# Dilated-attention keys and values to token rows: another queue for the value stores, four staging slots for keys, bias tables flipped in mid-stage

## The reference, cut to what matters

```python
logits = jnp.einsum('bqhd,bqkhd->bqhk', q, kk).astype(jnp.float32) * HEAD_DIM ** -0.5
logits = jnp.where(valid[None, :, None, :], logits + bias[None, None], -jnp.inf)
...
bufs = tuple(jnp.stack([k_a[:, -min(w, S):, g], v_a[:, -min(w, S):, g]], axis=2)
             for g, (w, _) in enumerate(DSA_GROUPS))
```

## Time and profile before

| | |
|---|---|
| runs (us) | 2523.01, 2510.16, 2494.77; median 2510.16 |
| profiled execution | 2512.98 us; span of its instructions 2511.2 us |
| busy share of the span | PE 89%, DVE 42%, ACT 21%, POOL 3% |
| mean granted TensorE clock | 0.913 |
| changed stage in the span | 377.6 to 402.1 us, some 24.5 us of 2511.2 |
| prompt attention behind it | 402.1 to about 530 us |

### The profile page before, as it was taken

The page is one execution under the profiler, slowest core; times in us unless marked ns, Lnnn a source line. Parts: engine busy times, 40 slices in busy tenths (PEclk is TensorE's granted clock), DMA queues, the critical chain, the costliest instruction groups (busy, mean ns, idle before and its releaser), DMA issues. The chain is left out here.

```text
span 2511.2 us, 40144 instructions
## 1 busy us (share of the span) xinstructions
PE 2228.1 (89%) x17448; PEld 1962.4 (78%) x17448; DVE 1061.6 (42%) x1398; ACT 523.0 (21%) x954; POOL 71.5 (3%) x129
## 2 busy tenths in 40 slices
PE   6999978957899788885899989777999999999997
PEld 6999966835577555554788888657999999999996
DVE  4212134565466577771222232566432432422433
ACT  3101004421333233230111121224111110111110
POOL 0000000000400011100000000000000000000000
PEclk8999957658899899996899999987999999999998
DMA  5113132031695378864211111301111111111111
GB/s 185 42 50 119 25 102 86 26 91 31 200 331 192 139 274 300 305 252 117 106 46 46 52 34 31 127 19 32 45 51 43 51 44 47 45 51 43 50 43 76
DMA packets 179012, 247.98 MB, mean 99 GB/s; under 512 B 23219, under 2 KB 164507, under 8 KB 173516
## 3 DMA queue, kind: packets, MB, share of 16 engines
q1 hardware_dynamic: 166992, 162.04, 20.8%
q0 software_dynamic: 5904, 83.95, 8.8%
q10 hardware_dynamic: 5996, 0.25, 0.2%
HBM read 220.35 MB, written 69.87 MB: 116 GB/s over the span
## 5 line engine op out<-in xcount | busy, mean ns | idle before, releaser
L1158 PE MATMUL ps<-mla_rt,q_now 32*32 32x256 f32 x4608 | 148.9, 396 | 48.5 <-DVE mla_rt L1252 44.3
L1252 DVE STREAM_TRANSPOSE mla_rt<-mla_rows 128x1536 f32<-128x1536 f32 x96 | 164.7, 1752 | 43.5 <-DMA mla_rows<-in_cache_mla,page_rows 43.0
L2306 PE MATMUL ps<-xn_hi,mlp_w_hi 128*128 128x344 f32 x768 | 164.1, 322 | 7.2 <-DVE mlp_w_lo L2120 5.3
L2306 PE MATMUL ps<-mlp_xn_lo,mlp_w_hi 128*128 128x344 f32 x768 | 163.7, 321 | 0.0
L1158 PEld LDWEIGHTS ps<-mla_rt,q_now 32*32 32x32 f32 x4608 | 97.1, 108 | 84.4 <-issue 63.1
L2306 PE MATMUL ps<-u_lo,mlp_w_hi 128*128 128x344 f32 x768 | 163.0, 320 | 0.0
L2306 PE MATMUL ps<-xn_hi,mlp_w_lo 128*128 128x344 f32 x768 | 162.9, 320 | 0.0
L2306 PE MATMUL ps<-u_hi,mlp_w_hi 128*128 128x344 f32 x768 | 162.9, 320 | 0.0
L2306 PE MATMUL ps<-u_hi,mlp_w_lo 128*128 128x344 f32 x768 | 162.1, 319 | 0.0
L2306 PEld LDWEIGHTS ps<-xn_hi,mlp_w_hi 128*128 128x128 f32 x768 | 129.7, 190 | 8.7 <-DVE mlp_w_lo L2120 6.4
L2306 PE MATMUL ps<-xn_hi,win_hi 128*128 128x344 f32 x576 | 123.3, 323 | 7.9 <-DVE win_lo L2571 7.9
(11 more groups left out here) (368 smaller groups left out, 3756.8 us busy)
## 6 DMA issues: line engine op xcount, KB each, us to landing
out_s_dsa_w<-in_cache_dsa_w SPq DMA_DIRECT2D x8, 4094.0 KB, 80.2
oaT<-in_w_up SPq DMA_DIRECT2D x32, 512.0 KB, 4.1
oaT<-in_w_down SPq DMA_DIRECT2D x32, 512.0 KB, 4.2
obT<-in_w_in SPq DMA_DIRECT2D x23, 512.0 KB, 3.7
gate_w<-in_w_in SPq DMA_DIRECT2D x16, 512.0 KB, 4.1
out_s_dsa_w<-in_cache_dsa_w SPq DMA_DIRECT2D x8, 1022.0 KB, 17.6
s_kv_tile<-in_cache_dsa_w SPq DMA_DIRECT2D x12, 512.0 KB, 5.5
x_scr<-qkvT SPq DMA_DIRECT2D x1, 4128.0 KB, 15.9
```

The source lines that it names most:

```text
L1158: last = nc.tensor.matmul(ps[32 * (JG * s + g):32 * (JG * s + g) + 32, i, 0:JN * SQ], q_now[SQ * i:SQ * i + SQ, s, c, :], rt[SQ * i:SQ * i ...
L1252: nc.vector.transpose(rt[:, k * n:(k + 1) * n], rows[:, v, :, k * n * SQ:(k + 1) * n * SQ].rearrange("p n (c f) -> p c n f", c=n)).then_in ...
L2306: last = nc.tensor.matmul(out[:, t, 0:TC], w, x[:, k, t * TC:(t + 1) * TC], start=first, stop=stop)
```

## The change

The value stores leave SyncE's queue for GpSimd's, with a semaphore of their own (`v_stored`), on which GpSimd waits in the merge at the end of the attention. The keys have four staging slots instead of two. The first four flips stand before unit 4's transposes and the fifth before unit 8's; the copies of the tables stand before ScalarE's copy of unit 5 (table 0), behind VectorE's second key copy (table 1), and before ScalarE's copy of unit 12 (tab2). The fifth flip uses the bank that the first table's copy has left.

```diff
+    v_stored = sem("v_stored")
...
-        kst = sb(st, "kst", [P, 2, GW])
+        kst = sb(st, "kst", [P, 4, GW])
...
-        k_stored = [sem("k_stored0"), sem("k_stored1")]
+        k_stored = [sem(f"k_stored{s}") for s in range(4)]
+        tab_moved = sem("tab_moved")
...
             @block.tensor
             def _(pe):
+                flip = mats[:, C_FLIP:C_FLIP + P]
                 for u, (g, i, q, _prev, _d) in enumerate(units):
                     if u >= 2:
                         pe.wait_ge(copied, u - 1)
+                    if u == 4:
+                        pe.wait_ge(tab_in, 16 * 3)
+                        for n in range(4):
+                            last = nc.tensor.matmul(ps[:, 2 + n, :], flip,
+                                                    sc[:, n // 2, 2 * (n % 2):2 * (n % 2) + 2, :].rearrange("p h n -> p (h n)"),
+                                                    start=True, stop=True)
+                        last.then_inc(flipped, 1)
+                    if u == 8:
+                        pe.wait_ge(tab_moved, 1)
+                        nc.tensor.matmul(ps[:, 2, :], flip, pt[:, 0, :, 0, :], start=True, stop=True).then_inc(flipped, 1)
...
-                flip = mats[:, C_FLIP:C_FLIP + P]
-                pe.wait_ge(tab_in, 16 * 3)
-                for n in range(4):
-                    nc.tensor.matmul(ps[:, 2 + n, :], flip, sc[:, n // 2, 2 * (n % 2):2 * (n % 2) + 2, :].rearrange("p h n -> p (h n)"),
-                                     start=True, stop=True).then_inc(flipped, 1)
-                pe.wait_ge(k_copied, len(kunits))
-                nc.tensor.matmul(ps[:, 6, :], flip, pt[:, 0, :, 0, :], start=True, stop=True).then_inc(flipped, 1)
             @block.scalar
             def _(act):
                 for u in range(NUN):
+                    if u == 5:
+                        act.wait_ge(flipped, 1)
+                        nc.scalar.activation(tab01[:, 0].rearrange("p h n -> p (h n)"),
+                                             ps[:, 2:4, :].rearrange("p a n -> p (a n)"), ACT.Copy).then_inc(tab_moved, 1)
+                    if u == 12:
+                        act.wait_ge(flipped, 2)
+                        nc.scalar.activation(tab2[:].rearrange("p h n -> p (h n)"), ps[:, 2, :], ACT.Copy)
                     act.wait_ge(turned, u + 1)
                     nc.scalar.activation(vtok[:, u, :], ps[:, u % 2, 256:512], ACT.Copy).then_inc(copied, 1)
-                for g in range(2):
...
-                act.wait_ge(flipped, 5)
-                nc.scalar.activation(tab2[:].rearrange("p h n -> p (h n)"), ps[:, 6, :], ACT.Copy)
             @block.vector
             def _(dve):
                 for n, u in enumerate(kunits):
                     dve.wait_ge(turned, u + 1)
-                    if n >= 2:
-                        dve.wait_ge(k_stored[n % 2], n // 2 * 16)
-                    nc.vector.tensor_copy(kst[:, n % 2, :], ps[:, 6 + n % 2, 0:GW]).then_inc(k_copied, 1)
+                    if n >= 4:
+                        dve.wait_ge(k_stored[n % 4], n // 4 * 16)
+                    nc.vector.tensor_copy(kst[:, n % 4, :], ps[:, 6 + n % 2, 0:GW]).then_inc(k_copied, 1)
+                    if n == 1:
+                        dve.wait_ge(flipped, 1)
+                        nc.vector.tensor_copy(tab01[:, 1].rearrange("p h n -> p (h n)"),
+                                              ps[:, 4:6, :].rearrange("p a n -> p (a n)"))
+            @block.gpsimd
+            def _(pool):
+                for u in kunits:
+                    g, i = units[u][:2]
+                    pool.wait_ge(copied, u + 1)
+                    pool.dma_start(rows_of(g, i, 1), vtok[:, u, :]).then_inc(v_stored, 16)
             @block.sync
             def _(sp):
...
                 for n, u in enumerate(kunits):
                     g, i = units[u][:2]
-                    sp.wait_ge(copied, u + 1)
-                    sp.dma_start(rows_of(g, i, 1), vtok[:, u, :]).then_inc(s_out, 16)
-                    n_out[0] += 1
                     sp.wait_ge(k_copied, n + 1)
-                    sp.dma_start(rows_of(g, i, 0), kst[:, n % 2, :]).then_inc(k_stored[n % 2], 16)
-                for s in range(2):
-                    sp.wait_ge(k_stored[s], 16 * ((len(kunits) + 1 - s) // 2))
+                    sp.dma_start(rows_of(g, i, 0), kst[:, n % 4, :]).then_inc(k_stored[n % 4], 16)
+                for s in range(4):
+                    sp.wait_ge(k_stored[s], 16 * ((len(kunits) + 3 - s) // 4))
...
+            @block.gpsimd
+            def _(pool):
+                pool.wait_ge(v_stored, 16 * len(kunits))
```

More of the change, by code:

```diff
@@ L392, in _ @@
                 for u in range(NUN):
+                    if u == 5:
[5 more added lines that the diff above has]
+                        nc.scalar.activation(tab2[:].rearrange("p h n -> p (h n)"), ps[:, 2, :], ACT.Copy)
                     act.wait_ge(turned, u + 1)
                     nc.scalar.activation(vtok[:, u, :], ps[:, u % 2, 256:512], ACT.Copy).then_inc(copied, 1)
-                for g in range(2):
-                    act.wait_ge(flipped, 2 * g + 2)
-                    nc.scalar.activation(tab01[:, g].rearrange("p h n -> p (h n)"),
-                                         ps[:, 2 + 2 * g:4 + 2 * g, :].rearrange("p a n -> p (a n)"), ACT.Copy)
-                act.wait_ge(flipped, 5)
-                nc.scalar.activation(tab2[:].rearrange("p h n -> p (h n)"), ps[:, 6, :], ACT.Copy)
             @block.vector
```

## The result

The change made the kernel slower by a little: 2513.82 us against 2503.32 us (medians of 20 runs each), 10.5 us apart. The ratio worked out from all these runs is 1.0036 with a 95% interval of 1.0023 to 1.0050, which is 9 us, between 6 and 12.5. The profiled execution spans 2519.1 us against 2511.2.

A forecast was written before the change was run, and what follows sets the result against it. Key slots and the flips at the end were taken to cost time in a stage of 24.6 of 2511.2 us. Wait 3.95, flips 5.15, units 4 to 16 +1.3, last leg -6.0 gave +4.4: 2514.5 us, range 2500 to 2528.

The forecast's parts named there:

- The wait at unit 4: TensorE stands at unit 4 until the third table load lands, wholly on the path: 3.95 us, bounds 3.6 and 4.45.
- Four flips: Eight flip instructions at unit 4, partly at half clock: 5.15 us, bounds 3.4 and 6.9.
- the rival: Half clock stays: four flips take 6.9 us, plus fifth flip and units 9 to 15; +7.8 in all, 2518; chance 0.10.
- Unit 4 to unit 16: Fifth flip and table copies lengthen this leg from 7.46 us to 8.8: +1.3, bounds +0.5 and +2.5.
- The last leg: Unit 16 to the next stage shrinks from 14.73 us to 8.7 with four slots: -6.0, bounds -7.6 and -4.8.
- eight units take 6.0 us: From unit 16 on, stores at 352 GB/s set the pace: 0.75 us a unit, so 6.0 us for eight.
- The sum: The four terms of the stage together: 3.95 + 5.15 + 1.3 - 6.0 = +4.4 us, bounds -0.1 and +9.05.
- The price of an issue: GpSimd gets thirteen value stores at 0.58 us a plain issue, keeping up with 0.75 us a unit.
- GpSimd ends the stage: Rival: issues of 1.24 us hold GpSimd at the barrier, +2.5 us more, +6.9 in all, 2517; chance 0.13.
- the bound at which bandwidth doesn't count: Unit 16 to the next stage if bandwidth didn't bind: 7.1 us, which gives -7.6.
- the attention would gain from a shifted clock: Rival: the attention behind the stage gains clock; with 20 us to full clock the sum is -5.6, 2504.6; chance 0.17.
- the change does less than it says: Rival: the keys' pace stays at 1.14 us, last leg only -2.5, sum +7.9, 2518; chance 0.05.

The follow-up runs named there:

- e3: The change with the value stores back on SyncE's queue: stage 30.7 us against the change's 31.3.
- e6: The change with the wait at unit 4 kept and the four flips there left out but for one narrow product: stage 26.9 us against the change's 31.3.
- e7: The change with five more flips of other data behind TensorE's last transposes, keeping it busy until the stage ends: stage 30.7 us against the change's 31.3.
- e5: The change with the four flips reading other data, so nothing is waited for at unit 4 (tables waited for at unit 8): stage 25.8 us against 31.3.
- e9: The change with flips before units 17, 19, 21, table copies on ScalarE, the last key stores waited for in the attention: stage 23.2 us, ratio to before 0.9987.
- e11: As e9, without the drain that GpSimd runs before the barrier at the stage's end: stage 20.6 us against e9's 23.2.
- e4: The change with the flips moved from units 4 and 8 to units 10 and 14, table copies moved along: stage 24.9 us against the change's 31.3.
- e10: As e9, with the value stores put back on SyncE's queue: stage 21.9 us against e9's 23.2.
- e2: The kernel before with four key slots alone, value stores on SyncE's queue and flips at the end: stage 21.2 us against 24.5, ratio 1.0004.
- e12: Thirteen key slots, no store waits in the stage, value stores at the attention's start, four value banks, flips at units 12, 16, 20: stage 18.5 us, ratio 0.9986.

## Why the prediction was right, and where its terms were off

**The hit on the total is in part luck.** 2514.5 us was forecast and 2513.8 measured, but the forecast started from 2510.2, the median of three runs, and the median of twenty is 2503.3. Added to that, +4.4 gives 2507.7. A base 6.8 us too high made up for an effect that was put too small. What was right by its mechanism is the sign (the flips' move costs more than the slots give back), the wait, and that it all stays within 1%.

**The wait at unit 4** was the term that decides, and it was there: 4.36 us instead of 3.95. The third load took 5.2 us to land, not 4.9; e3, e6 and e7 waited 4.1. TensorE ran nothing past it: no instruction in the 4.36 us, and unit 4's transposes only behind the flips. e5 shows that it is a cost by itself.

**Four flips** were put at 5.15 us, and the stretch took 5.96. The course was right (clock 0.50 from 382.92 to 388.70, then 1.00). The size of 3.35 us at half clock came from one row; here the clock came up 5.8 us into the flips, so nearly all of them ran at half clock, as the rival had it. The rival's price for them, 6.9 us, counted eight spacings of 0.86; counted between loads the first spacing is about 0.2. Its further terms did not come: from 388.88 on the clock was 1.00. But the same flips took 4.9 us in e3 and 5.7 in e7, both behind a stand-still, and 4.9 in e5 without one. So 5.15 lies within what the runs show, and what makes the clock rise sooner or later here stays open. The stand-still isn't needed for a slow start either: in the kernel before the clock was at 0.50 too from 377.50 to 383.00, past unit 4.

**Unit 4 to unit 16** took 8.15 us, +0.7 and not +1.3. Units 4 to 9 took 4.7 us (4.6 worked out) and units 10 to 15 3.5 (4.2): it is the copy to tab2 that hid better than worked out.

**The last leg** is the term that was sized worst: 10.5 us (397.03 to 407.50) and not 8.7, so it gave back 4.3 us and not 6.0. The step was "eight units take 6.0 us" at 352 GB/s, a rate read from a quarter of a microsecond. Over 397.03 to 401.00 it was 257 GB/s and then, to 404.30, 314. And the stretch moved 2.67 MB, where eight units are 2.10: stores of the units before unit 16 were still under way or not yet begun. Stores then landed in 2.9 to 3.1 us, so four slots filled up again (VectorE's last copy waited 1.48 us). That bandwidth would take over from the slots was right from 401.00 on (DMA share 0.97; before that 0.78). Behind the last landing the step had 0.3 us; 407.50 is 0.65 us behind the last key (404.75 and 2.1 us), because GpSimd was not at the barrier yet (below).

**The sum** of the four is 4.36 + 5.96 + 0.69 - 4.26 = +6.75 us for the stage (the wait is new, so it counts whole) where +4.4 was forecast. It lies inside the measured 6 to 12.5. Two more profiles of the same front, e3 and e7, have 6.2. The other 2 us are not settled: the attention was 2.6 us longer in this profile, but by e7 and the table that is within its own scatter.

**GpSimd's stores.** The price of an issue was near: 0.54 us for 0.58, thirteen times, with VectorE's key copies beside them, and the last of seven in a row (397.98 to 402.09) started 0.3 us behind its copy, so no backlog. The later wait costs nothing: GpSimd's last store landed at 406.68, and the merge starts at 537.5. What the prediction didn't have is the barrier's wait for GpSimd's landings (e9, e11). It costs little in the change, but it does set the end there. The last value store, issued at 403.58, landed after 3.1 us at 406.68, and the next stage started 0.8 us behind it, as in e4 to e9. The last key landed at 406.85, and in e3, where GpSimd has no stores, the next stage starts 0.4 us behind the last key (406.49 and 406.89). That would be 407.25, so the wait is worth some 0.25 us, an estimate from these rows. The rival named the right place (GpSimd ends the stage) with the wrong cause, issue time, and at ten times the price. With both queues at work, 401.00 to 404.30, GpSimd's took 52.8% of the 16 DMA engines and SyncE's 44.4%, together 0.97 at 314 GB/s; SyncE's alone had reached 1.03 and 352 GB/s before. So no road of its own shows for GpSimd: the last leg gave back 4.3 us, not the 7.6 of the bound at which bandwidth doesn't count. What its queue saves is issue time: that sets e3's last leg, 11.2 us against 10.5. In e10 and e11 the saving is seen again: 21.9 us against 20.6.

**The other rivals.** That the attention would gain from a shifted clock was given 0.17; with a scatter of 12 us between profiles it can be neither claimed nor excluded from one. That the change does less than it says is refuted: VectorE's waits for slots halved, and e2 shows 3.4 us for the slots.

## What to carry to other kernels

Before a wait is moved forward in an engine's list, read when its event lands, not when it was last needed: here a load that had been 12 us early became 4.4 us late, in which TensorE ran nothing at all, and the work moved so far forward ran at a lower clock as well (3.2 us for the same flips at unit 10 at 0.96, 6.0 at unit 4 in the change at 0.52). A bundle of three edits hid a good one (slots, -3.4 us of stage) under a bad one (flips, +10.4), which running each alone shows at once. Two runs that differ in one edit are best compared leg by leg: e3's stage was 0.6 us shorter than the change's while the leg that the edit touches was 0.8 us longer. And where stores go to GpSimd's queue, read its drain at the stage's end: here it waited for them, 3.2 to 3.7 us against 34 ns without stores, though the kernel asks for them only in the merge.

## What the runs showed of the hardware that was not expected

- With its drain, GpSimd joined the barrier only after its own stores had landed: the next stage started 0.8 us behind the last landing in e9 (395.5 + 2.6 = 398.1, end of the 3.18 us drain 398.7, start 398.91); without the drain it started 0.4 us behind ScalarE's last copy (395.65 and 396.06) and 0.07 us behind the end of GpSimd's last issue (395.99), which may be what held it. SyncE's outstanding stores didn't hold the barrier in e10: the stage ended 0.42 us after its last issue, which took 1.9 us to land, and SyncE's drain took 0.12 us.
- After 4.1 to 4.4 us without work TensorE's clock stayed at 0.50 until 3.7 (e3), 5.2 (e7) or 5.8 us (the change) into the same continuous flips; with work ahead of them it rose 3.7 us into the flips (e5).
- The same attention stage took between 118.0 and 130.0 us in fourteen profiles, its mean granted clock between 0.60 and 0.76. The code of its engines is the same but for waits and stores put into its SyncE list in e9 to e12. That scatter is larger than the 6.8 us of the change's stage.
